# Making the expert gates of a two-block layer: one pass of 128 activation slots and one of 128 value slots, all gates through DRAM

## The reference, cut to what matters

```python
PEER_HEADS, PEER_N_KEYS, PEER_TOPK = 8, 128, 16        # 16,384 experts
def peer_ffn(x, w_q, keys, u, v):                       # x: 256 tokens x 2048
    q = (xt @ w_q).reshape(T, PEER_HEADS, 2, PEER_KEY_DIM // 2)
    scores = jnp.einsum('thpd,pnd->thpn', q, keys)
    s_top, i_top = lax.top_k(scores, PEER_TOPK)
    cand = (s_top[:, :, 0, :, None] + s_top[:, :, 1, None, :]).reshape(T, PEER_HEADS, 256)
    cand_idx = (i_top[:, :, 0, :, None] * PEER_N_KEYS + i_top[:, :, 1, None, :]).reshape(...)
    s_fin, pos = lax.top_k(cand, PEER_TOPK)
    idx = jnp.take_along_axis(cand_idx, pos, axis=-1)
    gate = jax.nn.softmax(s_fin, axis=-1)
    # per token: y = sum over chosen experts e of  gelu(u[e] . x) * gate * v[e]
```

## Time and profile before

| | |
|---|---|
| median of 3 runs | 2941.63 us (2939.85 to 2941.86) |
| the profiled execution: its own time / span in the trace | 2941.99 us / 2940.2 us |
| PE busy | 2896.9 us, 99% |
| DVE, ACT, POOL busy | 1896.4, 1254.9, 651.0 us (64%, 43%, 22%) |
| HBM read and written | 530.69 MB and 19.01 MB, 187 GB/s |

### The profile page before, as it was taken

The page is one execution under the profiler, slowest core; times in us unless marked ns, Lnnn a source line. Parts: engine busy times, 40 slices in busy tenths (PEclk is TensorE's granted clock), DMA queues, the critical chain, the costliest instruction groups (busy, mean ns, idle before and its releaser), DMA issues.

```text
span 2940.2 us, 43202 instructions
## 1 busy us (share of the span) xinstructions
PE 2896.9 (99%) x16911; PEld 2565.5 (87%) x16911; DVE 1896.4 (64%) x2654; ACT 1254.9 (43%) x1467; POOL 651.0 (22%) x450
## 2 busy tenths in 40 slices
PE   8999999999999999999999999999999999999998
PEld 7888889988988889778999999988888888888886
DVE  5557677655666567756999788644446666654444
ACT  4336544544345344444444333334443334334344
POOL 0000034222000000000008777788870000000000
PEclk9999999999999999999999999999999999999999
DMA  5556545566554554344546555566667655555554
GB/s 215 193 193 248 205 149 177 204 211 233 191 186 174 200 187 158 141 155 168 178 177 185 144 144 144 173 186 199 187 198 253 233 187 192 191 187 197 187 199 172
DMA packets 125163, 551.45 MB, mean 188 GB/s; under 512 B 47344, under 2 KB 55664, under 8 KB 62320
## 3 DMA queue, kind: packets, MB, share of 16 engines
q1 hardware_dynamic: 70992, 513.95, 49.3%
q0 software_dynamic: 43008, 16.93, 3.7%
q10 hardware_dynamic: 11040, 18.88, 1.9%
HBM read 530.69 MB, written 19.01 MB: 187 GB/s over the span
## 4 chain that ended last, share of the span: by engine, by line
PE 94%; DVE 4%; ACT 1%; issue 0%; DMA 0%; ACTq 0%; SPq 0%; DVEq 0%
PE bank L551 25%; PE bank L1063 23%; PE bank L556 13%; PE bank L537 13%; PE bank L596 11%; PE bank L800 2%; PE bank L1040 1%; DVE wlo L1841 1%; PE bank L756 1%; ACT whi L1115 1%; PE bank L665 0%; PE bank L741 0%; DVE hT L1831 0%; PE bank L727 0%; PE bank L728 0%
## 5 line engine op out<-in xcount | busy, mean ns | idle before, releaser
L1841 DVE TENSOR_TENSOR wlo<-raw,whi 128x2048 fp32r<-128x2048 f32 (+1 forms) x484 | 1104.4, 2282 | 820.8 <-ACT whi L1115 819.7
L1115 ACT ACTIVATE whi<-raw 128x2048 fp32r<-128x2048 f32 (+1 forms) x484 | 921.3, 1904 | 1242.2 <-PE bank L551 512.4
L551 PE MATMUL bank<-hT,whi 128*128 128x512 f32 x3328 | 820.0, 393 | 2.5 <-DVE hT L1831 1.6
L1795 POOL DMA_INDIRECT gates_dram<-R x256 | 533.5, 2084 | 927.4 <-DVE R L2632 802.8
L551 PEld LDWEIGHTS bank<-hT,whi 128*128 128x128 f32 x3328 | 607.9, 188 | 118.6 <-DVE hT L1831 3.5
L537 PE MATMUL bank<-hT,whi 128*128 128x256 f32 x2304 | 447.3, 292 | 0.3 <-DVE wlo L1841 0.3
L556 PEld LDWEIGHTS bank<-hT,wlo 128*128 128x128 f32 x3328 | 426.4, 191 | 17.7 <-DVE wlo L1841 1.4
L556 PE MATMUL bank<-hT,wlo 128*128 128x256 f32 x3328 | 431.5, 283 | 0.9 <-DVE wlo L1841 0.9
L537 PEld LDWEIGHTS bank<-hT,whi 128*128 128x128 f32 x2304 | 356.2, 191 | 1.0 <-DVE wlo L1841 0.7
L537 PE MATMUL bank<-hT,wlo 128*128 128x256 f32 x1152 | 325.0, 282 | 0.0
L1063 PE MATMUL bank<-whi,ghi 128*128 128x512 f32 x1016 | 271.6, 389 | 0.0
(11 more groups left out here) (362 smaller groups left out, 2200.2 us busy)
## 6 DMA issues: line engine op xcount, KB each, us to landing
raw<-stream SPq DMA_DIRECT2D x484, 1024.0 KB
gates_dram<-token_scale POOLq DMA_DIRECT2D x128, 128.0 KB, 4.8
R<-cmpw ACTq DMA_DIRECT2D x16, 512.0 KB, 4.5
R<-gates_dram ACTq DMA_DIRECT2D x16, 512.0 KB, 5.6
gates_dram<-R POOLq DMA_INDIRECT x256
xres<-x SPq DMA_DIRECT2D x2, 1024.0 KB, 6.1
R<-mixw ACTq DMA_DIRECT2D x1, 1024.0 KB, 6.7
R<-fnw ACTq DMA_DIRECT2D x1, 1024.0 KB, 7.0
```

The costliest lines, as they stand in the source:

```text
L551: return mm(bank[to][:], whi[t][:, k * P:(k + 1) * P], hT2[:, k, :, :].rearrange("p a t -> p (a t)"), start=(at == 0), stop=(at == KC - 1))
L1115: A(whi[t][:, 0:w], raw[t][:, 0:w], ACT.Copy).then_inc(hi_ready[t], 1)
L1795: nc.gpsimd.indirect_dma_start(gates_dram, bass.IndirectOffsetOnAxis(ap=cell_u[:, b, c:c + 1], axis=0), chosen[:, b, 2, c:c + 1], None, co ...
L1841: V.tensor_tensor(wlo[t][:, 0:w], raw[t][:, 0:w], whi[t][:, 0:w].bitcast(F32), ALU.subtract).then_inc(raw_free[t], 1)
```

## The change

The two halves become one: `peer_u` has 128 slots, all of `t2_slot`; `peer_v` has 128 slots of `expert_values`. PE makes no gates. All gates go through DRAM by POOL's indirect adds; the one-hot rows, `token_gates`, `weigh`, `keep_gates`, `gate_made` and `add_experts` are gone. The choice goes head by head (both blocks of tokens at once) in 8 parts, one per slot, from the fourth query slot on: 64 slots, the last of them slot 50 of `peer_u`. POOL can add the gates of a head as soon as it is chosen, 32 transfers per head with one wait. ACT stores the activations of the first 64 slots to DRAM (256 KB for each pair of slots) and keeps the others. From slot 122 of `peer_u` on, when all adds have landed, ACT loads tiles of 128 KB: one of gates for each value slot, and for the first 64 value slots one of activations. DVE multiplies them (`product`), ACT and DVE split the product.

```diff
-          ("peer_u0", 16), ("peer_v0", 16), ("peer_u1", 16), ("peer_v1", 16)]
+          ("peer_u", 32), ("peer_v", 32)]
...
+CHOOSE_FIRST = 3
+PARTS = 8
+SCALED_AT = {n: n // 2 - 1 for n in range(2, NK, 2)}
+SPILLED = HALF // 2
+TILES = 4
+TILES_AT = NK - 6
+def part_of(n):
+    h, q = divmod(n - CHOOSE_FIRST, PARTS)
+    return (h, q) if n >= CHOOSE_FIRST and h < PH else (0, None)
...
             for s in range(RING):
-                t_slot("peer_u0", 0, s, lambda k: key_scores(2 * PH - 2 + s) if s < 2 and k == KC // 2 else None)
-            phase_t("peer_u0", 1, CHOOSE_G - 1)
...
+                t2_slot("peer_u", 0, s, middle=(lambda: key_scores(2 * PH - 2 + s)) if s < 2 else None)
+            with pe.Fori(1, G0["peer_u"][1]) as i:
+                for s in range(RING):
+                    t2_slot("peer_u", i, s)
...
+            for slot in range(NK):
+                if slot + 1 < NK:
+                    split("peer_u", *divmod(slot + 1, RING))
...
+                exp_gates(2 * PH + slot)
...
                 if slot in SCALED_AT:
-                    gelu_early(SCALED_AT[slot])
...
+                    gelu_pair(SCALED_AT[slot])
+                elif 0 <= (slot - 3) // 2 < SPILLED and slot >= 3:
+                    spill_pair((slot - 3) // 2)
+                if slot == TILES_AT:
+                    act.wait_ge(scattered, 16 * TB * HK)
...
+            with act.Fori(1, n // 2 - 1) as i:
+                for s in range(RING):
+                    split("peer_v", i, s)
+                    high_acts(i, s)
+                    next_tile(i, s, True)
...
-            for b in range(TB):
-                pool.wait_ge(chosen_ready, b + 1)
-                pool.wait_ge(cells_known, b + 1)
-                for h in range(PH):
-                    for c in range(h * TOPK, (h + 1) * TOPK):
+            for h in range(PH):
+                pool.wait_ge(head_chosen, h + 1)
+                for k in range(TOPK):
+                    for b in range(TB):
                         nc.gpsimd.indirect_dma_start(
-                            gates_dram, bass.IndirectOffsetOnAxis(ap=cell_u[:, b, c:c + 1], axis=0),
-                            chosen[:, b, 2, c:c + 1], None, compute_op=ALU.add).then_inc(scattered, 16)
-                    pool.wait_ge(scattered, 16 * (b * HK + (h + 1) * TOPK))
+                            gates_dram, bass.IndirectOffsetOnAxis(ap=cell_u[:, b, h, k:k + 1], axis=0),
+                            gate_of[:, b, h, k:k + 1], None, compute_op=ALU.add).then_inc(scattered, 16)
+                pool.wait_ge(scattered, 16 * TB * TOPK * (h + 1))
...
+            for slot in range(NK):
                 if slot > 0:
-                    sum_acts(0, slot - 1)
+                    sum_acts(slot - 1)
                 if slot in SCALED_AT:
-                    scale_acts(0, SCALED_AT[slot])
...
+                    scale_acts()
+                if slot + 1 < NK:
+                    split("peer_u", *divmod(slot + 1, RING))
                 else:
-                    split("peer_v0", 0, 0)
...
+                    split("peer_v", 0, 0)
+                choose(*part_of(2 * PH + slot))
...
+            def value_slots(i, src, at, last=None):
+                for s in range(RING):
+                    split("peer_v", i, s)
+                    low_acts(i, s)
+                    if s < RING - 1:
+                        product(i, s + 1, src, at + s + 1)
```

More of the change, by code:

```diff
@@ L454, in turn_again, with acts @@
             return 2 if n == 2 and f < 4 else 8 if n == 2 else 4
[L456 to L466, removed]
+        def acts(i, s):
+            return i * 2 + (s // 2 + 1)
         def bc(ap, shape):
@@ L1602, in _ @@
                 else:
-                    split("peer_u0", 0, 0)
+                    split("peer_u", 0, 0)
+                exp_gates(n)
                 if n == 2:
@@ L1626, in _, with gelu_pair @@
-            for slot in range(EARLY):
-                split("peer_u0", *divmod(slot + 1, RING))
+            def gelu_pair(p):
+                act.wait_ge(acts_scaled, p + 1)
+                if p >= SPILLED:
+                    at = 2 * (p - SPILLED)
+                    A(late[:, at:at + 2, :].rearrange("p j t -> p (j t)"), act_in, ACT.Gelu).then_inc(gelu_done, 1)
+                    return
+                if p >= 2:
+                    act.wait_ge(spilled[p % 2], 16 * (p // 2))
+                A(spill[p % 2], act_in, ACT.Gelu).then_inc(gelu_done, 1)
@@ new lines, in _ @@
+            for s in range(2):
+                high_acts(0, s)
+                next_tile(0, s, True)
+            split("peer_v", 0, 1)
+            gelu_pair(NK // 2 - 1)
+            for s in range(2, RING):
+                split("peer_v", 0, s)
+                high_acts(0, s)
+                next_tile(0, s, True)
+            with act.Fori(1, n // 2 - 1) as i:
[3 more added lines that the diff above has]
+                    next_tile(i, s, True)
@@ new lines, in _ @@
+            for s in range(RING):
+                split("peer_v", n // 2 - 1, s)
+                high_acts(n // 2 - 1, s)
+                next_tile(n // 2 - 1, s, s == 0)
+            with act.Fori(n // 2, n - 1) as i:
+                for s in range(RING):
+                    split("peer_v", i, s)
+                    high_acts(i, s)
+                    next_tile(i, s, False)
+            for s in range(RING):
+                split("peer_v", n - 1, s)
+                high_acts(n - 1, s)
+                next_tile(n - 1, s, False, s == 0)
@@ L2642, in _ @@
                 else:
-                    split("peer_u0", 0, 0)
+                    split("peer_u", 0, 0)
                 evac_one("wq", *divmod(n - 1, RING))
-                if n >= 3:
-                    key_rows(n - 3)
+                choose(*part_of(n))
             evac_one("wq", *divmod(2 * PH - 1, RING))
@@ new lines, in _ @@
+                    scale_acts()
+                if slot + 1 < NK:
+                    split("peer_u", *divmod(slot + 1, RING))
+                else:
+                    split("peer_v", 0, 0)
+                choose(*part_of(2 * PH + slot))
+            n = G0["peer_v"][1]
+            for s in range(2):
+                product(0, s, act_tile, s)
+            for s in range(2):
+                low_acts(0, s)
+            sum_acts(NK - 1)
+            scale_acts()
+            product(0, 2, act_tile, 2)
@@ new lines, in _ @@
+            split("peer_v", 0, 1)
+            for s in range(2, RING):
+                split("peer_v", 0, s)
+                low_acts(0, s)
+                product((s + 1) // RING, (s + 1) % RING, act_tile, (s + 1) % RING)
+            def value_slots(i, src, at, last=None):
+                for s in range(RING):
+                    split("peer_v", i, s)
+                    low_acts(i, s)
+                    if s < RING - 1:
+                        product(i, s + 1, src, at + s + 1)
+                    elif last is None:
+                        product(i + 1, 0, src, at + RING if src is late else at)
+                    elif last is late:
+                        product(i + 1, 0, late, 0)
@@ L2865, in layout @@
         cols_n(i["w_out_2"][0]), cols_t(i["peer_w_q_2"][0]),
-        *(w[half * HALF:(half + 1) * HALF] for half in range(2) for w in (peer_u, peer_v))])
+        peer_u, peer_v])
     t = np.arange(T)
```

539 lines of the change are left out of this document (151 added, 388 removed).

## The result

The changed kernel takes **2872.57 us** (median of 4 runs, 2870.95 to 2873.13), against 2941.72 us of the kernel before in the same comparison (4 runs, 2939.85 to 2941.86). The ratio is 0.9765, with a 95% interval of 0.9749 to 0.9782. That is 69.15 us less; the forecast was 68.8 less, 2873 us, in a range of 2870 to 2890.

The account below looks back on a forecast made before the run. PE was taken to bound the kernel, a slot costing what its matmuls cost. Terms -68.2 - 0.9 + 0.3 = -68.8 us, others 0, took the median-based 2941.6 to 2872.8, so 2873 us, range 2870 to 2890.

Parts of the forecast that it names:

- Slots of the first half: First 64 activation slots on PE take the form of the old peer_u1: 357.3 in place of 425.5 us, -68.2 us.
- Border of the stages: Between peer_u and peer_v: add_experts goes, -0.9 us; PE waits for one product more before the first value slot, +0.3 us.
- DVE in choosing slots: 51 activation slots where DVE also chooses: about 5.4 us a slot, under PE's 5.57, backlog covered, 0 us.
- ACT and the table changes: ACT in activation slots: 3.4 us idle a slot; exponential once in 8 slots, two table changes of 1.28 us; 0 us.
- The adds: POOL's 256 adds: 2.57 us each while DVE chooses, then 2.8; last lands near 2110, before ACT's wait matters; 0 us.
- The margin: ACT's wait for the adds at slot 122 may last until 2139: free by 29 us, by 2 at the slow end.
- Tiles in the value slots: Value slots: 256 KB more per slot in half of them, and DVE's product, cost PE 0 us.
- The Trainium skill: On POOL's adds beside DVE's split: by its rule every add costs 1.84 us, last head in by 1800; prediction sided against.
- The likeliest rival, DVE too full: Choosing slots: DVE can't choose and sum at once; 5.8 us a slot costs 7 us, at worst 29; 2880 to 2902; chance 0.12.
- The slower rival: ACT's wait at slot 122: last add landing after 2208 makes the kernel slower than before, 2999 at 3.3 us each; chance 0.02.

Follow-up runs that it names:

- the two additions: The changed kernel with 14 of 16 matmuls per peer_u slot split in two: 2891.98 us; separately, with 248 products of 64 columns put back: 2932.5 us.
- the first of the two kernels: The changed kernel with one more DVE sum of 512 elements in each of the 51 choosing slots of peer_u: 2884.97 us.

## Why the prediction was right, point by point

- **Slots of the first half**, -68.2: right. PE's borders are where forecast to 0.2 us, and the two additions put 65 to 73 us on the work removed. That both forms of slot stood whole in the trace made the prediction safe.
- **Border of the stages**, -0.9 + 0.3: right; 0.35 us are left. (The terms that the prediction lists for it add up to 5.9 us and not to the 5.8 it writes, so to 0.4.)
- **DVE in choosing slots**, 5.37 us each at no cost: right; 5.32 measured. The estimate by width for 1024 elements held (1.22 against 1.23). The rival gave 7 us for 5.8 us a slot; by its own formula the 5.92 of the first of the two kernels (5.32 and 0.60) would give 51 x 0.35 - 4.4 = 13.5, and 12.4 were measured.
- **ACT and the table changes**, 0: right. In the waits from 1450 to 2860 us, where DVE's split waits for `whi` 401.4 us, ACT itself stands almost only for a free buffer behind PE (397.6 and 404.8 us, with 9.9 us for DVE's scaling as the next), and never for a load.
- **The adds**, cost 0: right, but the term was mis-sized. It said that while DVE chooses I take 2.57 each, and that the last lands near 2110. Measured at the ends of batches, the first 128 needed 1766.74 - 1421.17 = 345.6 us, 2.70 each; the rest kept the forecast pace, 89.1 us for 32 (1855.62 to 1944.77), 2.8 each. Part of both is idle time of POOL that no wait in the trace explains: 3.7, 4.1 and 5.0 us before the adds at 1573.97, 1722.19 and 1745.14, and 2.5, 2.2 and 2.7 us before three later ones. These are always the 61st, 114th, 121st, 181st, 227th and 241st add, in every kernel here that has the adds, that of before included. So it hangs on the number of the add and not on DVE or on the time; every 60th and every 113th would fit. What POOL does there stays open. The margin was 17 us (four slots earlier, 22.3 us, PE stands for 4.8), not 29.
- **Tiles in the value slots**, 0: right. With 32 MB more it is 4 to 6 us.
- **The Trainium skill** (SBUF — State Buffer, Who interferes with whom) infers that a `tensor_tensor` doesn't hold back descriptor writing. The runs show the whole add, as POOL's instruction, held behind that very instruction: halving it moved the last add by 144 us. They don't part the writing of its descriptors from its reading of gates and cells in SBUF, and the same section says that a VectorE instruction with two inputs in SBUF contends with a GpSimd instruction that reads SBUF; the 3.29 us fit that sentence, so the page speaks less against the rows than the prediction has it. The rule that the engine that starts first blocks the other for its whole instruction is stated there for VectorE's two-port modes. For `tensor_tensor` against an add it holds one way only: without any adds DVE's busy time and the time of the kernel stayed.

The likeliest rival, DVE too full, had the right mechanism and failed by a margin of 0.25 us a slot. The slower rival (last add after 2208) was 85 us away. That the late adds stayed inside their margin was in part luck: the pace of 2.57 us came from another mix of slots, the margin was little over half of the one forecast, and the forecast did not know that the pace jumps with the slot's length.

No version here beats the changed kernel. PE is busy all but 0.2 us of the activation and value slots, so what is left to gain there lies in PE's own slots, and not in the covers. The kernel with the split in two is worth knowing, since it takes as long and has 144 us more room on POOL. An intermediate kernel, with the new slots and the old choice, wasn't built, so what the choice by heads gives alone isn't measured. Nor is the storing and loading of activations tried by itself; the windows and waits show only that PE doesn't wait for it.

## What to carry to other kernels

When one engine is busy in every window, price a change by its slots: find the old and the new form of a slot as a whole in the trace, multiply, and then spend the effort on the covers (how far ahead a split is made, when a wait is reached against when its event comes), each with a number for the point at which it gives out. Small products between long matmuls were dear here: two passes of 64 columns cost 0.24 us, as much as a matmul of 512 (0.23). And where a wait has a deadline, move it towards the event in two steps: that measures the cover directly.

## What the runs showed that was not expected

- An add that starts inside a DVE operation on two operands in SBUF ends 1.4 us after that operation (up to 3.66 us for 1.54); the reverse isn't so (DVE 265.97 us busy with adds, 265.08 without). Two instructions of half the length let 256 adds end 144 us earlier.
- A stop of PE of 4.8 us was followed by matmuls at 0.44 us in place of 0.24, a granted clock of 0.63 in the window after it and 2.8 us lost on top; one of 35.8 us lost 2.2 on top. In these two the extra didn't grow with the stop.
- A late DVE split shows up as ACT's waiting for loads, 117 us in all, because the same instruction frees the buffer.
- The same six adds of the 256 have 1.76 to 5.05 us of idle time before them in every kernel with adds, whatever DVE does; the cause stays open.
